# GpSimd's weight split in quarters: four roundings and four subtractions of 256 columns in turn, in place of one and one of 1024

## The reference, cut to what matters

```
hp = rms_norm(xp, norm_g[i]) * (1.0 + sc_p) + sh_p
hs = rms_norm(xs, norm_g[i]) * (1.0 + sc_s) + sh_s
...
q, k, v, z = jnp.split(h @ w_in, ...)
...
return (o.reshape(B, S, -1) * jax.nn.silu(z)) @ w_out
```

## Time and profile before

| | |
|---|---|
| median of 3 runs | 2256.95 us (2256.05 to 2260.66) |
| the profiled execution: its own time | 2252.97 us |
| its span in the profile | 2251.2 us |
| busy: PE / DVE / ACT / POOL | 2058.2 / 1177.5 / 803.4 / 547.6 us |
| mean granted clock of TensorE | 0.948 of full speed |

### The profile page before, as it was taken

The page is one execution under the profiler, slowest core; times in us unless marked ns, Lnnn a source line. Parts: engine busy times, 40 slices in busy tenths (PEclk is TensorE's granted clock), DMA queues, the critical chain, the costliest instruction groups (busy, mean ns, idle before and its releaser), DMA issues.

```text
span 2251.2 us, 34991 instructions
## 1 busy us (share of the span) xinstructions
PE 2058.2 (91%) x14168; PEld 1765.2 (78%) x14168; DVE 1177.5 (52%) x2309; ACT 803.4 (36%) x1824; POOL 547.6 (24%) x440
## 2 busy tenths in 40 slices
PE   6999998889999997979979999998997989999888
PEld 4887886878989886968957868687876977888677
DVE  5477665563555553576534323241161666777544
ACT  5365554123444443031132232313221035555432
POOL 1313200433233311334310111102112542222122
PEclk8999998989999998979979999999998989999889
DMA  9212122322223223134222334325236221102001
GB/s 330 56 49 78 51 59 80 89 59 80 66 81 98 63 62 115 38 51 154 81 61 71 91 121 103 94 87 143 93 96 132 68 77 30 51 2 69 20 20 57
DMA packets 302286, 181.53 MB, mean 81 GB/s; under 512 B 59557, under 2 KB 276910, under 8 KB 302126
## 3 DMA queue, kind: packets, MB, share of 16 engines
q1 hardware_dynamic: 283860, 158.39, 24.0%
q10 hardware_dynamic: 18266, 20.90, 4.1%
HBM read 153.51 MB, written 25.74 MB: 80 GB/s over the span
## 4 chain that ended last, share of the span: by engine, by line
PE 75%; DVE 9%; ACT 8%; DMA 3%; issue 3%; SPq 1%; ACTq 1%; POOL 0%; DVEq 0%; POOLq 0%
PE pc L1682 20%; PE acc L1608 12%; PE acc L710 5%; PE acc L1774 4%; PE acc L1763 4%; PE pt L1785 3%; PE acc L700 3%; PE pc L765 3%; PE pt L710 2%; PE acc L1992 2%; PE acc L2004 2%; DMA out_mlstm_n<-amat 1%; PE acc L654 1%; PE pt L2012 1%; PE acc L1938 1%
## 5 line engine op out<-in xcount | busy, mean ns | idle before, releaser
L1523 POOL TENSOR_TENSOR idle<-eps 128x1 f32<-128x1 f32 x144 | 38.1, 264 | 1637.8 <-PE pc L765 306.0
L1682 PE MATMUL pc<-hh,wh 128*128 128x320 f32 x1152 | 380.0, 330 | 16.7 <-DVE hl L2661 8.2
L1526 POOL TENSOR_TENSOR wl<-raw,wh 128x1024 fp32r<-128x1024 f32 x144 | 368.0, 2556 | 11.5
L1682 PE MATMUL pc<-hl,wh 128*128 128x320 f32 x1152 | 362.1, 314 | 0.0
L1682 PE MATMUL pc<-hh,wl 128*128 128x320 f32 x1152 | 361.9, 314 | 0.0
L1682 PEld LDWEIGHTS pc<-hh,wh 128*128 128x128 f32 x1152 | 221.8, 192 | 29.0 <-issue 15.7
L1682 PEld LDWEIGHTS pc<-hl,wh 128*128 128x128 f32 x1152 | 222.8, 193 | 0.2 <-issue 0.2
L1682 PEld LDWEIGHTS pc<-hh,wl 128*128 128x128 f32 x1152 | 221.9, 193 | 0.0
L2283 ACT COPY ht<-pt 128x512 f32<-128x512 f32 (+1 forms) x160 | 76.4, 525 | 214.8 <-PE pt L1785 214.6
L1524 POOL CAST wh<-raw 128x1024 fp32r<-128x1024 f32 x144 | 150.9, 1048 | 0.0
L1774 PE MATMUL acc<-ht,gvt 128*64 128x128 f32 x1344 | 100.7, 298 | 19.3 <-ACT ht L2288 14.9
(11 more groups left out here) (386 smaller groups left out, 4437.6 us busy)
## 6 DMA issues: line engine op xcount, KB each, us to landing
raw<-in_w_mod SPq DMA_DIRECT2D x144, 256.0 KB, 3.4
raw<-in_gqa_w_in SPq DMA_DIRECT2D x80, 256.0 KB, 3.6
raw<-in_diff_w_in SPq DMA_DIRECT2D x64, 256.0 KB, 3.8
raw<-in_mlstm_w_in SPq DMA_DIRECT2D x64, 256.0 KB, 3.4
praw<-in_w_mod SPq DMA_DIRECT2D x32, 256.0 KB, 9.9
raw<-in_gqa_w_out SPq DMA_DIRECT2D x32, 256.0 KB, 3.2
out_mlstm_C<-amat ACTq DMA_DIRECT2D x16, 512.0 KB, 7.4
raw<-in_mlstm_w_out SPq DMA_DIRECT2D x32, 256.0 KB, 3.1
```

Source lines behind the costliest of these rows:

```text
L1526: pool.tensor_tensor(wl[:, s], raw[:, r], wh[:, s].bitcast(F32), ALU.subtract).then_inc(w_full[s], 1)
L1682: ins = pe.matmul(pc[:, c:c + 320], w[:, sl, kt, :], h[:, kt, t:t + 320], start=kt == 0 and n == 0, stop=kt == KT - 1 and n == 2)
```

## The change

Each panel's one rounding and one subtraction of 1024 columns become four of each on 256 columns (two of the eight feature tiles). The order is: rounding of quarter 0, rounding of quarter 1, subtraction of quarter 0, rounding 2, subtraction 1, rounding 3, subtraction 2, subtraction 3. Each subtraction waits for the rounding of its own quarter alone. `w_full` still comes once, with the last subtraction, and no other engine's instructions are touched.

```diff
-                pool.tensor_copy(wh[:, s], raw[:, r]).then_inc(pool_step, 1)
-                pool.wait_ge(*seen(pool_step))
-                pool.tensor_tensor(wl[:, s], raw[:, r], wh[:, s].bitcast(F32), ALU.subtract).then_inc(w_full[s], 1)
+                rounded = []
+                for k in range(0, KT, 2):
+                    pool.tensor_copy(wh[:, s, k:k + 2], raw[:, r, k:k + 2]).then_inc(pool_step, 1)
+                    rounded.append(seen(pool_step))
+                    if k:
+                        pool.wait_ge(*rounded[-2])
+                        pool.tensor_tensor(wl[:, s, k - 2:k], raw[:, r, k - 2:k], wh[:, s, k - 2:k].bitcast(F32), ALU.subtract)
+                pool.wait_ge(*rounded[-1])
+                pool.tensor_tensor(wl[:, s, KT - 2:KT], raw[:, r, KT - 2:KT], wh[:, s, KT - 2:KT].bitcast(F32), ALU.subtract).then_inc(w_full[s], 1)
```

## The result

The changed kernel takes 2235.77 us (median of 4 runs, 2234.63 to 2236.61) against 2258.71 us for the kernel before (4 runs): a ratio of 0.9902, interval 0.9887 to 0.9917, or 22 us faster. Timed once more beside other kernels, it gave 0.9901 (0.9874 to 0.9929). The prediction was 2250 us with a range of 2243 to 2259: the side was right, the size was off by a factor of three. In the two traces TensorE's waits shrink by 10.8 us, where the prediction's sum had 6.9; the rest of the 22 us lies in its busy time, for which the sum had no term.

What follows compares the result with a forecast made beforehand. TensorE, busy 91% of the span, was taken as the bound, so only its waits counted; gains and costs summed to -6.9 us, taking the runs' median from 2256.95 to 2250 us, range 2243 to 2259.

Steps and rivals of the forecast that it cites:

- five waits behind L2766: Attention: VectorE's L2766 waits for a quarter instead of a whole rounding; TensorE's five waits there shrink by 2.2 us.
- L2962 at the end of layers 0 and 2: VectorE's L2962 starts after one more quarter, not a whole subtraction; TensorE's two waits shrink by 1.6 us.
- first head of the mLSTM: Twelve short L1099 each meet one of sixteen pieces, losing 4.8 to 6.4 us against 5.2 before: -0.3 us.
- heads two to four: Later mLSTM heads: L1099 gains about 0, three L1150 lose less, -0.6 a head; L600's waits shrink by 1.5 us.
- norm before the mLSTM: Seven dense VectorE operations meet six or seven pieces before `hl` is made; TensorE's 6.33 us wait grows by 0.5.
- norm of layer 0: Two splits, each 0.5 us longer, reach about 1 us into the dense norm: a cost of 0.6 us.
- late transfer: The one place where TensorE waits for a split, behind a late transfer: the longer split costs 0.5 us.
- the rule for dense places: Where VectorE is dense it waits once per quarter met, gaining only with fewer instructions than the split has pieces.
- the slower rival: GpSimd gives up no turn between back-to-back pieces, so a split holds VectorE 4.2 us: +26 us, 2283; chance 0.09.
- The price of a quarter: On GpSimd, 0.34 us per quarter rounding and 0.72 per subtraction between starts; a split takes 4.2 us against 3.7.
- Hidden work: Rival: TensorE waits that end earlier uncover others right behind, so only about -2 us, 2255; chance 0.30.
- Dear pieces: Rival: six more GpSimd instructions eat the 2.6 us spare in the mLSTM's output: +8 us, 2265; chance 0.06.

Runs made afterwards that it cites:

- again: The kernel before, unchanged, timed and profiled once more: 2260.03 us, ratio 1.0015.
- eighths: The change's alternating order with pieces of 128 columns instead of 256: 2229.68 us, ratio 0.9881 to the kernel before.
- eighths_own: Against the change, pieces of 128 columns, each subtraction right behind its own rounding and waiting for it: 2244.30 us, ratio 0.9943 to the kernel before.
- own_wait: Against the change, each quarter's subtraction stands right behind its own rounding and waits for it: 2232.88 us, ratio 0.9893 to the kernel before.
- halves: The change's alternating order with pieces of 512 columns instead of 256: 2239.06 us, ratio 0.9922 to the kernel before.
- sub_only: Against the kernel before, only the subtraction cut into four of 256 columns, the rounding left whole: 2238.52 us, ratio 0.9918.

## Why the prediction was wrong in size

The trace after was laid over that of before matmul by matmul; both executions had a granted clock of 0.948, and their spans differ by 16.4 us. What changed in the gaps ahead of TensorE's matmuls, the first one's included (us):

| term of the sum | predicted | in the traces |
|---|---|---|
| five waits behind L2766 | -2.2 | -2.6 |
| L2757 in layer 3 | -1.5 | -1.4 |
| two more L2757 | -1.4 | -1.8 |
| L2962 at the end of layers 0 and 2 | -1.6 | -1.4 and +4.7 |
| first head of the mLSTM | -0.3 | -1.1 |
| heads two to four | -1.5 | -5.6 |
| norm before the mLSTM | +0.5 | -0.2, and +0.5 at its next wait |
| norm of layer 0 | +0.6 | +0.5 at its first wait, -0.9 behind it |
| late transfer | +0.5 | +0.8 |
| L1818, three places; L776, seven places | not in it | -1.7 and -2.2 |
| all other gaps | | +1.6 |
| sum of the gaps | -6.9 | -10.8 |
| TensorE's busy time, 2058.2 to 2052.7 | not in it | -5.5 |
| span | | -16.4 |

**The step that failed** is the sum itself: it holds TensorE's waits alone and so puts any change of its busy time at nothing, without a reason. The waits moved by 10.8 us where 6.9 were forecast; from 2256.95 that alone would have made 2246. The other half of the 22 us is no wait: 5.5 us of busy time between these two traces, and some 5 to 6 more between them and the executions on the whole. Over the traces kept here TensorE's busy time falls as the granted clock rises, from 2066.9 us at 0.942 (again) to 2044.1 at 0.954 (eighths), with a scatter of some 5 us at like clocks. These two traces have the same mean clock, but the lower clock falls on other matmuls: one of layer 0's norm at 48 us takes 0.30 us before and 0.47 after. What shifts the clock, and what gives the change a little more of it, isn't shown.

**The term that was most mis-sized** among the waits is heads two to four, by the rule for dense places: "Where VectorE is dense it waits once for each quarter that it meets", and from it "about 0" for L1099 and "-0.6 a head". L1099 itself bore it out, with 5.08 us for twelve before and now, in the second head:

```profile
1000.54 5.15 DVE L1099 TENSOR_TENSOR bd<-mc,wsm 128x128 f32<-128x128 f32 x12 [3.60 <-ACT r L886]
```

For the first three long L1150 it was far off: I charged 1.0 to 1.4 us, and the trace has 0.16 (2.90 against 2.74). The 0.9 for what follows was about right, 0.48 (L1148) and 0.38, but the next three L1150 had lost 0.84 before as well (3.58 against 2.74), and I left that out. A long operation of VectorE has its place while a quarter waits, and the quarter's turn seems to fall largely into what passes between two such operations anyway. So L600's wait of 1.88 us went at each of three heads, where I had put 0.5.

**Left out.** TensorE's waits at L776 named ScalarE (9.6 us at seven places before, 7.4 at six after), and those at L1818 named no releaser and are gone; I took only waits that named VectorE or stood beside a row of it. In the waits before:

```profile
PE acc L776 <- ACT amat L1001: 9.6, 7, 1.8
...
PE pt L1818 <- issue: 1.7, 3, 0.9
```

That VectorE's hold reached them through the engine named is the likely way, but it wasn't traced instruction by instruction.

**L2962.** The mechanism was right at layer 0 and on the mean (2422 to 1048 ns); at layer 2 the slower rival's mechanism took the turn and gave back 4.7 us. I had given that rival 0.09 as a state of the whole kernel; it is one of single arrivals. In the Trainium skill (GPSIMD Engine Reference, section 2.1) a core begins the next instruction when its own share is done; the prediction drew from this that no turn might be given up at all, and the traces show that it mostly is.

**The price of a quarter** was right: predicted 0.34 and 0.72 between starts, measured 0.36 and 0.67. A split beside nothing takes 4.15 us, predicted 4.2. On the mean of all 144 it takes 4.7 against 3.7, twice the predicted 0.5 more, because VectorE's turns now fall into it. The Trainium skill's table (GPSIMD Engine Reference, section 3.1) had led to an estimate of 0.61 for the subtraction; the measured price lies between. (Four times the 0.11 between 0.72 and 0.61 are 0.44, not the 0.3 of the prediction; its sum doesn't use it.)

**The base.** I set 2246 against the profiled 2252.97 and added the 4 us by which the median lay above it. Those 4 us go with the clock: 0.948 in the profiled execution, 0.946 on the mean of 43 executions of before, whose mean span is 2254.9 us (standard deviation 3.8). Ten executions of the change have 2233.1 us at 0.948. Span times clock is 2133.6 (standard deviation 3.3) and 2117: 17 less, or some 17.5 us at this clock, near the 16.4 of the two traces. By this reckoning, which is rough, the other 4 us of the 22 go with the higher mean clock.

**The other rivals.** Hidden work (2255) falls: waits that ended earlier uncovered nothing of their size. Dear pieces (2265) don't come with quarters: TensorE waits for GpSimd once, as before; they come with the sixteen pieces and eight waits of eighths_own.

None of the versions is better than the change by more than the intervals allow; own_wait has the whole gain, and its trace shows no missed turn and the least idle time of TensorE, 161.3 us.

## What to carry to other kernels

Where two engines take turns at instruction length, cut the instructions of the engine that has time to spare, the long one first: the other loses the rest of a piece, not of a panel. Stop before the pieces' fixed time makes the work late: 256 columns did it here, and so did 128 without waits; 128 with a wait each did not. Price a dense stretch from what its own long instructions lose beside short pieces, not at a full piece for each instruction, and look behind waits that name a third engine. Before a gain is put down to waits, take the bounding engine's idle and busy time apart: here the waits were only half of it.

## What the hardware showed that was not expected

- With GpSimd's pieces back to back, VectorE mostly gets its turn behind the piece in front, yet now and then misses it for a whole split: 4.79 and 4.88 us in the change, 3.87 with roundings and subtractions in order. With 0.08 us of idle time ahead of every second piece no such case appeared, but none did in halves and sub_only either, which have no such gaps. What decides a missed turn, the gap or the moment of arrival, stays open; at the end of layer 2 it came in all three traces with this order of quarters there.
- The mean granted clock differs between kernels with the same matmuls: 0.946 for before, 0.948 for the change, 0.953 for eighths (4 executions) and 0.952 for eighths_own (6). In the trace of eighths_own TensorE is idle for 179.9 us, 3.4 longer than before, and yet its mean span is 2243.0 against 2254.9; span times clock is 2134, the same as of before. Here none of the gain is in waits; it goes with the clock. What raises the clock isn't shown.
